# Seven products of the identity with itself ahead of the first values of each sparse-attention round

## What is computed

```python
o_cmp = p_c @ v_cmp        # over compressed blocks
o_sel = p_s @ v_g          # over selected blocks of 64 positions
o_win = band_attention(q_rot, k_win, v_win)     # over a window of 128
o = gates[0] * o_cmp + gates[1] * o_sel + gates[2] * o_win
```

## Time and profile before

| what | value |
|---|---|
| timed executions | 2623.76, 2628.63, 2632.39 us |
| time of the profiled execution | 2625.72 us |
| its span, first to last instruction | 2623.9 us |
| mean granted TensorE clock | 0.974 of full speed |
| TensorE busy | 2530.9 us (96%) |
| VectorE busy | 1406.4 us (54%) |
| ScalarE busy | 1329.6 us (51%) |
| GpSimd busy | 774.8 us (30%) |

### The profile page before, as it was taken

One profiled execution on the slowest core, in us unless ns is written; L12 is line 12 of the kernel. 1 busy time (PEld: TensorE's weight loads), 2 busy tenths in 40 slices (PEclk: granted clock), 3 DMA queues, 4 the chain that ended last, 5 costly groups with the idle time before them and its releaser, 6 DMA issues. The chain is left out here.

```text
span 2623.9 us, 50014 instructions
## 1 busy us (share of the span) xinstructions
PE 2530.9 (96%) x17489; PEld 2469.0 (94%) x17489; DVE 1406.4 (54%) x2213; ACT 1329.6 (51%) x1998; POOL 774.8 (30%) x810
## 2 busy tenths in 40 slices
PE   6999999999999998999999999999999998889998
PEld 6999998999999986999999998999999996679997
DVE  6455456554555466645455456555455456755543
ACT  4565444664466336555365332565465344755642
POOL 2333233332233222333133224333133211113331
PEclk8999999999999998999999999999999998879999
DMA  6234443444344440443444433443444463114442
GB/s 224 88 129 146 146 156 116 159 145 153 141 156 144 145 181 1 145 156 140 152 147 157 149 143 127 155 149 136 152 160 144 149 225 119 55 46 153 151 141 104
DMA packets 66305, 366.24 MB, mean 140 GB/s; under 512 B 9154, under 2 KB 21762, under 8 KB 28290
## 3 DMA queue, kind: packets, MB, share of 16 engines
q1 hardware_dynamic: 64530, 356.58, 38.0%
q0 software_dynamic: 1536, 4.20, 0.5%
q10 hardware_dynamic: 144, 4.19, 0.4%
HBM read 361.98 MB, written 4.92 MB: 140 GB/s over the span
## 5 line engine op out<-in xcount | busy, mean ns | idle before, releaser
L295 ACT ACTIVATE w_hi<-w_raw 128x1024 fp32r<-128x1024 f32 (+1 forms) x641 | 657.6, 1036 | 747.4 <-PE bank L322 718.4
L322 PE MATMUL bank<-x_hi,w_hi 128*128 128x320 f32 x3336 | 1036.0, 311 | 0.0
L322 PE MATMUL bank<-x_lo,w_hi 128*128 128x320 f32 x3336 | 1030.8, 309 | 0.0
L322 PE MATMUL bank<-x_hi,w_lo 128*128 128x320 f32 x3336 | 1030.8, 309 | 0.0
L304 DVE TENSOR_TENSOR w_lo<-w_raw,w_hi 128x1024 fp32r<-128x1024 f32 (+1 forms) x641 | 832.6, 1334 | 259.3 <-ACT w_hi L295 259.3
L322 PEld LDWEIGHTS bank<-x_hi,w_hi 128*128 128x128 f32 x3336 | 626.3, 188 | 2.1 <-issue 0.6
L322 PEld LDWEIGHTS bank<-x_hi,w_lo 128*128 128x128 f32 x3336 | 626.3, 188 | 1.3
L322 PEld LDWEIGHTS bank<-x_lo,w_hi 128*128 128x128 f32 x3336 | 626.2, 188 | 0.0
L322 PE MATMUL bank<-h_hi,w_hi 128*128 128x320 f32 x1664 | 518.2, 311 | 14.2 <-POOL h_lo L925 6.5
L322 PE MATMUL bank<-h_hi,w_lo 128*128 128x320 f32 x1664 | 516.6, 310 | 0.0
L322 PE MATMUL bank<-h_lo,w_hi 128*128 128x320 f32 x1664 | 516.5, 310 | 0.0
(11 more groups left out here) (292 smaller groups left out, 2065.0 us busy)
## 6 DMA issues: line engine op xcount, KB each, us to landing
w_raw<-stream SPq DMA_DIRECT2D x289, 1024.0 KB, 4.8
w_raw<-stream SPq DMA_DIRECT2D x32, 768.0 KB, 4.1
n_sel<-pool_sel SPq DMA_DIRECT2D x64, 128.0 KB, 2.1
w_raw<-cmp_w SPq DMA_DIRECT2D x4, 1024.0 KB, 9.1
pages<-pool_cmp SPq DMA_DIRECT2D x32, 128.0 KB, 5.2
pages<-pool_cmp POOLq DMA_DIRECT2D x32, 128.0 KB, 5.2
w_new<-cmp_w ACTq DMA_DIRECT2D x1, 4096.0 KB, 15.3
const<-const SPq DMA_DIRECT2D x1, 1533.0 KB, 11.1
```

What stands on the lines that cost most here:

```text
L295: act.activation(w_hi[:, (2 * n + half) % HALVES, 0:k, :], raw[:, n % RAW, 0:k, P * half:P * half + P], ACT.Copy).then_inc(hi_ready, 2 if ...
L322: mm = pe.matmul(acc, w[:, s, kk, :], a[:, k0 + kk, :], start=(first and kk == 0 and w is w_hi and a is act_hi), stop=(last and kk == k - ...
```

## The change

A new function issues products of the identity matrix (128x128, float32) with itself into a given output. In `values`, the wait for `no_lo` now comes first; for unit 0 seven such products into bank 7 follow it; then comes the wait for `npt_copied`, which stood first before. The first real product into the bank has `start=True`, so what the seven left is overwritten.

```diff
+        def keep_clock(pe, out, count):
+
+            for _ in range(count):
+                pe.matmul(out[:, 0:P], cst("ident"), cst("ident"), start=True, stop=True)
...
             def values(V, u, r, k):
-                pe.wait_ge(npt_copied, V)
                 pe.wait_ge(no_lo, V - 1)
                 out = bank[7][:, 0:P]
+                if u == 0:
+                    keep_clock(pe, out, 7)
+                pe.wait_ge(npt_copied, V)
```

## The result

The changed kernel takes 2643.16 us (median of five, 2642.74 to 2645.81) against 2626.75 us of the kernel before (median of five, 2623.42 to 2632.39). The ratio is 1.0065, 95% interval 1.0054 to 1.0077: **slower by 0.65%**, some 17 us.

What follows compares the result with a forecast made beforehand. Rounds were taken to wait for VectorE's release of bank 7, with VectorE setting the pace in short clock falls. Products +11.3, clock -2.7 and -0.5, slow products +1.55 gave +9.6 us: 2628.6 to 2638.2 us, range 2630.5 to 2645.5.

Steps and rivals of the forecast that it cites:

- rival 4: In the loop, the clock falls ahead of the products in most rounds, so they run at 1.2 GHz: +17.5 us; chance 0.06.
- One group of products at full clock: Ahead of unit 0's values: seven products, 14 instructions 0.111 us apart, cost 1.55 us, uncovered in rounds 1 to 7.
- Products at half clock: In one loop round of seven the products run at 1.2 GHz and cost 1.55 us more.
- What the clock gives back in the loop: Most long clock falls go, returning 2.7 us, and some of the short falls return 0.5 us.
- The bound of that return: A full clock in the loop returns at most 3.5 us: 2 x 1.35 for long falls, 5 x 0.15 for short.
- Round 0: In the first round the products run inside its 1.14 us wait, leaving 0.4 us of their 1.55 us as cost.
- Behind the last round: From the last round to the projection, the clock stays as it is: no change taken, between -5 and +2 us.
- Rival 1: In and behind the loop, products hold 2.4 GHz and return half the half-clock time, 25.9 us: -14.5 us; chance 0.04.
- Rival 2: Within 0.3%: all long falls go and the loop's end gets part of its clock back, +4.8 us; chance 0.34.
- Rival 3: In the loop, the clock falls in every round as before, so only the products' cost shows: +11.3 us; chance 0.15.

Runs made afterwards that it cites:

- the ends: Products added to the kernel before only in waits ahead of the loop and in and behind its last round: 2621.06 us, ratio 0.9982.
- the fastest kernel: Kernel before plus seven bank 4 products inside every round's wait and groups in waits ahead of the loop and in and behind its last round: 2616.85 us, ratio 0.9964.

## Why the prediction was right, and where it was short

**The sign and the mechanism held.** The text said that the products cannot start before bank 7 is free, that the wait therefore stays and the products follow it, and that neither ScalarE nor VectorE has work for that time. All three are shown: by the timeline, by the grown waits of both engines, and by the two kernels with bank 4, one with the products behind the wait and one with them inside it. The predicted 2638.2 us is 5 us below the measured 2643.2, within the range of 2630.5 to 2645.5.

That closeness has luck in it. The forecast stood on the median of three executions, 2628.6 us; the five of the result have 2626.75, and 9.6 us more than that is 2636.4. The upper end of the range, +17 us, was there for rival 4, and the measured 16 to 17 us reach it for other reasons: rival 4's half-clock products would add 6.2 us, and they added 2.1. The forecast's rounds of some 18.1 us came out at 17.6 to 21.8 us.

**The size was short:** 9.6 us against 17.0 between the profiled executions, or some 15.3 without the 1.67 us lost before the attention. Term by term:

- *One group of products at full clock*: 1.55 us predicted, 1.76 measured. The step from one instruction to the next, 0.111 us, was right. Left out was what a group costs by starting and ending, 0.2 us. Over seven rounds this is 1.5 us.
- *Products at half clock*: +1.55 us predicted, +2.1 measured (14.40 less 7 x 1.76), in four rounds, each in part.
- *What the clock gives back in the loop*: -3.2 us predicted, +0.85 measured. This is the largest error of the sum, "I take most long falls as gone". Falls came in the middle of a group of products or at its end: at 2248.9 for products that began at 2247.91, at 2269.4 for products from 2267.90. Behind the products come the small values and the turn, and there the clock stayed at 0.50 for 6.8 and 10.2 us. The second profile of the same kernel lost less there, so the size of this term is not one number.
- *The bound of that return*: 3.5 us predicted, 4.7 measured with fourteen products (120.1 less 115.4). A short fall was put at 0.15 us by VectorE's wait of round 1. Laid beside the same round with fourteen products, that one lost 0.06 us, rounds 3 and 4 lost 0.2 us each, and the two long ones 1.3 and 1.4. But round 0 (17.53 us, against 16.80) and round 6, the one before the last values (16.55 us, against 15.82 from 2336.10 to 2351.92), lost 0.7 us each with a short fall too, so one round was too thin a base.
- *Round 0*: +0.4 us predicted, +0.65 measured.
- *Ahead of the loop*: nothing predicted, +1.8 us measured in this profile. As shown above, 1.67 us of it were lost before the attention and are not the change's. The second profile of the same kernel has +0.2 us there.
- *Behind the last round*: nothing predicted, +0.05 and -0.7 us measured.

**The rivals.** Rival 1, faster by 14.5 us because half-clock time is lost time, is refuted by its own best case: with the clock at 0.97 in the loop 2.3 us came back, not 12. The timed executions say the same of the whole program. Of the 26 of the kernel before that were timed beside the experiments with three and ten products and with the ends, the fastest took 2622.19 us at a mean clock of 0.980 and the slowest 2635.03 us at 0.968. That is some 64 us more at half clock for 12.8 us, a fifth and not a half. Rival 2 needed the end of the loop to get its clock back. From the last values to the projection the first profile of the changed kernel had a clock of 0.70, where it was 0.54 before, and took as long (16.35 us against 16.30); the second was at half clock throughout. This stretch became 2.2 and 2.6 us shorter when products were put there, and at most 1.3 us shorter without (15.04 us with the seven inside the wait). Rival 3, no effect on the clock, was nearest to what the first profile shows (27 us at half clock against 31), and its +11.3 us was short by what a group costs more, by the half-clock products, by the 0.85 us that the rest grew, and by the 1.67 us lost ahead of the attention. Rival 4, products at half clock in four rounds, names the nearest number, +17.5 us, but its mechanism holds for a third of its price.

What stays open is why the clock falls where it does. The runs show few or no falls in the loop with dense work within the rest (0.97, 0.97 and 1.00 in three kernels), and that the same work behind it does not prevent them reliably (0.90 and 0.96 in two profiles of one kernel). Why one kernel keeps its pattern and another does not was not settled.

## What to carry to other kernels

Filler work helps only if it can run while the engine waits: it must be ahead of the wait in the engine's order, need nothing that the wait is for (here the bank), and be no longer than the wait. Read a slow clock by what is late because of it: compare the same round at both clocks before putting a price on it. Put filler first where the slow work is itself on the path, here dense products ahead of and behind the loop, and not where another engine sets the pace. In the fastest kernel some 34 us less at half clock ahead of and behind the loop came with 7.2 us less time (2.0, 2.6 and 2.6), and 24 us less within the loop with 2.3.

## What was not expected

The half-clock time in the loop varies with the loop's own work unchanged, and one profile of each kernel does not tell what it follows. With the two waits exchanged it was 19 us, with only the ends filled 40 us (a clock of 0.84 over 125.0 us), and in the kernel before 31 us twice. The kernel with the ends filled was 0.18% faster than the kernel before by the ratio, and its profile is no typical one for it: it is of the slowest of twelve executions, 2627.94 us at a mean clock of 0.975 over the whole program. The fastest, 2614.49 us, had 0.984. One profile of a kernel whose clock varies so much can mislead, and the times and mean clocks of all its executions tell whether it does.
